# Splitting the last inner chunk and the last LayerNorm into 352 and 192 tokens instead of 256 and 288

## What is computed

```python
ALPHA = (2.0 * DEPTH) ** 0.25
def layer_norm(x, g, b):
    mu = jnp.mean(xf, axis=-1, keepdims=True)
    var = jnp.mean(jnp.square(xf - mu), axis=-1, keepdims=True)
    return (xf - mu) * lax.rsqrt(var + LN_EPS) * g + b
def squared_relu_mlp(x, w_up, w_down):
    return jnp.square(jax.nn.relu(x @ w_up)) @ w_down
...
xp = layer_norm(ALPHA * xp + mp, ln1_g[i], ln1_b[i])
xp = layer_norm(ALPHA * xp + squared_relu_mlp(xp, mlp_w_up[i], mlp_w_down[i]), ln2_g[i], ln2_b[i])
```

## Time and profile before

| | us |
|---|---|
| three runs | 1057.39, 1058.70, 1059.36; median 1058.7 |
| the profiled execution | 1058.65 |
| its span in the profile | 1056.8 |
| PE busy (share of the span) | 1040.4 (98%) |
| DVE busy | 839.9 (79%) |
| ACT busy | 661.7 (63%) |
| POOL busy | 226.9 (21%) |

### The profile page before, as it was taken

The page is one execution under the profiler, slowest core; times in us unless marked ns, Lnnn a source line. Parts: engine busy times, 40 slices in busy tenths (PEclk is TensorE's granted clock), DMA queues, the critical chain, the costliest instruction groups (busy, mean ns, idle before and its releaser), DMA issues.

```text
span 1056.8 us, 20704 instructions
## 1 busy us (share of the span) xinstructions
PE 1040.4 (98%) x8247; PEld 1017.4 (96%) x8247; DVE 839.9 (79%) x1283; ACT 661.7 (63%) x1159; POOL 226.9 (21%) x285
## 2 busy tenths in 40 slices
PE   8999999999999999999999999999999999999996
PEld 8999999999999999999999878999999999999995
DVE  6999898979779697696974664888879697696885
ACT  5999858665736647463666775675836647457432
POOL 2111032011111111103344564210111111111023
PEclk9999999999999999999999999999999999999997
DMA  7423214477877877865131211164777977878402
GB/s 256 121 91 100 81 60 138 104 159 160 176 167 159 200 160 160 203 174 185 40 121 47 67 58 39 41 180 81 159 169 158 199 161 161 201 162 175 134 12 75
DMA packets 54479, 139.83 MB, mean 132 GB/s; under 512 B 5632, under 2 KB 21440, under 8 KB 54368
## 3 DMA queue, kind: packets, MB, share of 16 engines
q0 software_dynamic: 14512, 53.60, 29.5%
q1 hardware_dynamic: 39584, 84.32, 23.9%
q10 hardware_dynamic: 288, 0.59, 0.2%
HBM read 135.95 MB, written 3.56 MB: 132 GB/s over the span
## 4 chain that ended last, share of the span: by engine, by line
PE 81%; DVE 9%; ACT 5%; issue 3%; POOL 1%; DMA 1%; SPq 0%; DVEq 0%; ACTq 0%; POOLq 0%
PE bank L2472 8%; PE bank L2491 8%; PE bank L2493 8%; PE bank L2473 8%; PE bank L2474 8%; PE bank L2492 8%; PE bank L2217 5%; PE bank L2218 5%; PE bank L2219 5%; PE bank L2304 3%; PE bank L2305 3%; PE bank L2306 3%; DVE w_lo L1348 2%; PE bank L2612 1%; PE bank L2586 1%
## 5 line engine op out<-in xcount | busy, mean ns | idle before, releaser
L834 ACT ACTIVATE w_hi<-stage 128x1024 fp32r<-128x1024 f32 x164 | 168.2, 1053 | 125.4 <-DMA stage<-w_up 67.8
L1354 DVE TENSOR_TENSOR w_lo<-stage,w_hi 128x1024 fp32r<-128x1024 f32 x164 | 197.1, 1220 | 54.0 <-ACT w_hi L834 54.0
L2491 PE MATMUL bank<-part_hi,w_hi 128*128 128x272 f32 x672 | 194.7, 290 | 0.4 <-issue 0.4
L2493 PE MATMUL bank<-part_hi,w_lo 128*128 128x272 f32 x672 | 194.2, 289 | 0.0
L2492 PE MATMUL bank<-part_lo,w_hi 128*128 128x272 f32 x672 | 193.3, 288 | 0.0
L2217 PE MATMUL bank<-x_hi,w_hi 128*128 128x288 f32 (+1 forms) x496 | 145.3, 293 | 1.4 <-issue 1.0
L2218 PE MATMUL bank<-x_lo,w_hi 128*128 128x288 f32 (+1 forms) x496 | 143.7, 290 | 0.0
L2219 PE MATMUL bank<-x_hi,w_lo 128*128 128x288 f32 (+1 forms) x496 | 143.1, 288 | 0.0
L2491 PEld LDWEIGHTS bank<-part_hi,w_hi 128*128 128x128 f32 x672 | 126.4, 188 | 1.7 <-issue 0.6
L2492 PEld LDWEIGHTS bank<-part_lo,w_hi 128*128 128x128 f32 x672 | 126.7, 189 | 0.0
L2493 PEld LDWEIGHTS bank<-part_hi,w_lo 128*128 128x128 f32 x672 | 126.7, 189 | 0.0
(11 more groups left out here) (292 smaller groups left out, 2912.5 us busy)
## 6 DMA issues: line engine op xcount, KB each, us to landing
stage<-w_up SPq DMA_DIRECT2D x54, 512.0 KB, 3.7
stage<-w_down SPq DMA_DIRECT2D x52, 512.0 KB, 4.2
stage<-w_down POOLq DMA_DIRECT2D x48, 512.0 KB, 5.4
stage<-w_up POOLq DMA_DIRECT2D x44, 512.0 KB, 5.5
stage<-w_qkv SPq DMA_DIRECT2D x10, 512.0 KB, 4.5
stage<-w_x SPq DMA_DIRECT2D x8, 512.0 KB, 5.1
stage<-w_y SPq DMA_DIRECT2D x8, 512.0 KB, 3.5
stage<-w_out SPq DMA_DIRECT2D x8, 512.0 KB, 3.3
```

Source lines behind the costliest of these rows:

```text
L834: A(w_hi[:, slot_of(l, k), :], raw_of(l, c, k), ACT.Copy).then_inc(s_whi, 1)
L1354: vt.tensor_tensor(w_lo[:, s, :], raw_of(l, c, k), w_hi[:, s, :].bitcast(F32), ALU.subtract)\
L2491: mm(out, wh, xh[:, k, :], start=(fresh and k == 0), stop=False, skip_group_check=True)
L2493: ins = mm(out, wl, xh[:, k, :], start=False, stop=(k == 1), skip_group_check=True)
```

## The change

`FINAL` gives halves of 352 and 192 columns, and `span(L, h)` returns them for the last LayerNorm (`L == 3`) and for the last chunk of layer 1's MLP, which counts as `L = 2 * l + (c > 0)`; everywhere else `HALF` stays. The tiles used in that stage are new, since 352 columns do not fit the old ones: they lie over the upper halves of `m_hi` and `m_lo`, over `z` and over `sq`. The column form of the last statistics goes in two blocks of 96 tokens instead of three.

```diff
 HALF = [(0, 256), (256, TOK - 256)]
 HW = TOK - 256
+FINAL = [(0, 352), (352, TOK - 352)]
+FC, FW = FINAL[1]
+FROWS, FCOLS = 96, 2
+def span(L, h):
+    return FINAL[h] if L == 3 else HALF[h]
...
-        fin = place("fin", [96, 12], F32, t_at["u"])
-        diag = place("diag", [96, 3, 96], F32, t_at["u"] + 64)
+        fin = place("fin", [FROWS, 12], F32, t_at["u"])
+        diag = place("diag", [FROWS, FCOLS, FROWS], F32, t_at["u"] + 64)
...
+        wide = FINAL[0][1]
+        h_at, l_at = t_at["m_hi"] + m_half, t_at["m_lo"] + m_half
+        sums_f = [[place("sum_c", [128, wide], F32, t_at["z"]), place("sumsq_c", [128, wide], F32, t_at["z"] + 4 * wide)],
+                  [sums[1][0], sums[1][1]]]
+        relu_f = place("relu_f", [128, 2, wide], F32, h_at)
+        h_sq_f = place("h_sq_f", [128, 2, wide], F32, h_at + 8 * wide)
+        mean_f = place("mean_f", [128, wide], F32, h_at + 16 * wide)
+        rstd_f = place("rstd_f", [128, wide], F32, h_at + 20 * wide)
+        msq_f = place("msq_f", [128, wide], F32, l_at)
+        red_hi_f = place("red_hi_f", [128, 2, wide], F32R, l_at + 4 * wide)
+        red_lo_f = place("red_lo_f", [128, 2, wide], F32R, l_at + 12 * wide)
+        sqt_f = place("sqt_f", [128, 2, wide], F32, t_at["sq"])
+        def wide_or(L, mine, usual):
+            return mine if L == 3 else usual
...
             def down(l, c, h, w0):
-                t0 = turn_of(l, c) * 8 + 4 * h + 2
-                width = HALF[h][1]
+                t0, L = turn_of(l, c) * 8 + 4 * h + 2, 2 * l + (c > 0)
+                width = span(L, h)[1]
...
             def up(l, c, h, w0, ts=range(4)):
                 for t in ts:
                     n0 = up_unit(l, c, h, t)
                     loop_bank(l, n0)
-                    product(n0, HALF[h][1], quad_pieces(w0, t, h))
+                    product(n0, span(2 * l + (c > 0), h)[1], quad_pieces(w0, t, h, L=2 * l + (c > 0)))
...
             pe.wait_ge(s_diag, 1)
-            for b in range(3):
-                ins = mm(bank[:, root_bank, 96 * b:96 * b + 96], ones[0:96, :], diag[:, b, :], start=True, stop=True)
+            for b in range(FCOLS):
+                ins = mm(bank[:, root_bank, FROWS * b:FROWS * b + FROWS], ones[0:FROWS, :], diag[:, b, :], start=True, stop=True)
             ins.then_inc(s_finroot, 1)
```

More of the change, by code:

```diff
@@ L977, in square @@
             def square(L, h, m):
-                c0, n = HALF[h]
+                c0, n = span(L, h)
                 pos = tile_pos(L, h, m)
@@ L983, in square @@
                     act.wait_ge(s_s2, pos - 1)
-                A((sqt_late if L == 2 else sqt)[:, pos % 2, :n], acc[:, m, c0:c0 + n], ACT.Square).then_inc(s_sqt, 1)
+                A(wide_or(L, sqt_f, sqt_late if L == 2 else sqt)[:, pos % 2, :n], acc[:, m, c0:c0 + n], ACT.Square).then_inc(s_sqt, 1)
             square(0, 0, 0)
@@ L995, in norm_stats @@
             def norm_stats(L, h):
-                _, n = HALF[h]
+                _, n = span(L, h)
                 m0 = mark[("ln", L, h)]
@@ L1000, in norm_stats @@
                     act.wait_ge(s_xhat, 4 * idx)
-                A(mean[:, :n], unit(m0)[:, :n], ACT.Copy).then_inc(s_evA, 1)
+                A(wide_or(L, mean_f, mean)[:, :n], unit(m0)[:, :n], ACT.Copy).then_inc(s_evA, 1)
                 act.wait_ge(s_var, idx + 1)
-                A(rstd[:, :n], msq[:, :n], ACT.Sqrt).then_inc(s_std, 1)
+                A(wide_or(L, rstd_f, rstd)[:, :n], wide_or(L, msq_f, msq)[:, :n], ACT.Sqrt).then_inc(s_std, 1)
             def sum_hi(L, h, part):
-                _, n = HALF[h]
+                _, n = span(L, h)
                 no = sum_no(L, h, part)
@@ L1012, in sum_hi @@
                     act.wait_ge(s_redlo, no - 1)
-                A(red_hi[:, part, :n], sums[h][part][:, :n], ACT.Copy).then_inc(s_redhi, 1)
+                A(wide_or(L, red_hi_f, red_hi)[:, part, :n], sums_of(L, h)[part][:, :n], ACT.Copy).then_inc(s_redhi, 1)
             def norm_apply(L, h, beside=lambda t: None):
-                c0, n = HALF[h]
+                c0, n = span(L, h)
                 idx = 2 * L + h
@@ L1640, in norm_apply @@
                            after_root=lambda: None):
-                c0, n = HALF[h]
+                c0, n = span(L, h)
                 idx = 2 * L + h
+                mean_now, rstd_now = wide_or(L, mean_f, mean), wide_or(L, rstd_f, rstd)
                 def pair(a, t):
@@ L2068, in add_square @@
             def add_square(L, h, m):
-                _, n = HALF[h]
+                _, n = span(L, h)
                 pos = tile_pos(L, h, m)
-                s2 = sums[h][1]
-                squares = sqt_late if L == 2 else sqt
+                s2 = sums_of(L, h)[1]
+                squares = wide_or(L, sqt_f, sqt_late if L == 2 else sqt)
                 pool.wait_ge(s_sqt, pos + 1)
@@ L2451, in down @@
                     loop_bank(l, down_unit(l, c, h, m))
-                    product(down_unit(l, c, h, m), width, down_pieces(w0 + 4, m, h))
+                    product(down_unit(l, c, h, m), width, down_pieces(w0 + 4, m, h, L))
             def up(l, c, h, w0, ts=range(4)):
```

121 lines of the change are left out of this document (66 added, 55 removed).

## The result

The changed kernel took 1061.8 us, the median of six runs (1060.2 to 1063.3), against 1058.6 us for the kernel before (1057.4 to 1059.4, six runs): ratio 1.0038, 95% interval 1.0028 to 1.0048. It is slower, by 3.1 us.

What follows compares the result with a forecast made beforehand. PE, on the chain for 81% of the span, was taken as the bound. Terms 8.1 - 2.3 - 2.6 = +3.2 us on 1058.7 gave 1061.9 us, range 1061.1 to 1063.1, widened for rivals to 1059.9 to 1064.0.

Steps and rivals of the forecast that it cites:

- rival D: Second half's narrow products fall to another pace, up to 0.50 us each: +71, total up to 1135 us; chance 0.05.
- Step 1: Last chunk's first half, 256 to 352 columns: 0.161 us per product, +8.1 us (7.9 to 8.4).
- Step 2: Last chunk's second half, 288 to 192 columns: weight load holds products at 0.112 us (ends 0.090 and 0.119).
- rival A: Second half's narrow products keep the slope, 0.090 us, the load hidden: total +1.9, 1060.6 us; chance 0.13.
- Step 3: Second half: PE waits 0.8 us for the sums, about 1 us at the fourth down slab; net gain -2.3 us.
- Rival B: Second half: DVE's stretch shorter, only PE's pace and first wait count; gain -3.3, total +2.2, 1060.9 us; chance 0.14.
- Rival C: Both halves: products at 0.090 us, no wait for DVE, only the shorter tail left: 1056.1 us; chance 0.06.
- Step 4: After the last product: narrower statistics, scaling and transfer shorten the tail by -2.6 us (-2.0 to -3.1).

Runs made afterwards that it cites:

- early-up kernel: Changed kernel (352/192) with the second half's last up tile handled by DVE and ACT before the LayerNorm's last three multiplications: 1059.6 us, ratio 1.0018.
- The series 288, 304, 320, 352: Last-chunk halves of 288/256, 304/240, 320/224 (last up tile earlier) and 352/192 (changed kernel): ratios to the kernel before 0.9992, 0.9997, 0.9996, 1.0038.
- 240-column kernel: Changed kernel with second-half products padded from 192 to 240 columns, the extra results unread: 1061.2 us, ratio 1.0031 to the kernel before.
- kernel before with the early up tile: Kernel before (256/288) with only the last up tile handled ahead of the LayerNorm's last three multiplications in the second layer: ratio 1.0003.
- 304/240 with the early up tile: Against the kernel before: halves of 304 and 240 columns, last up tile ahead of the LayerNorm's last three multiplications: 1057.1 us, ratio 0.9994.

## Why the prediction came out as it did

The forecast was +3.2 us, 1061.9; the measured median is 1061.8, and from the start of the chunk to the end the profile gives +3.0. The sum is right to 0.2 us, and its large terms, the first half and the second, were each right to 0.4. Two smaller ones behind the last product were off, in opposite directions, so that the closeness is in part luck; on the chip of the experiments the medians are 4.0 us apart. The working has small slips that change nothing: the ends of its terms add up to +2.5 and +4.5 and not +2.4 and +4.4, the chances to 0.98, and the 0.75 us in the earlier trace rows with which rival D prices one plain matmul is that of two.

*Step 1, first half.* Forecast +8.1 (7.9 to 8.4), measured 30.53 - 22.83 = +7.7. The pace is 0.159 and not the 0.161 I took: the slope of 0.00045 us per column, read between 256 and 288, is too steep. From 288 to 352 it is (0.159 - 0.133)/64 = 0.0004, about one column per cycle at 2.4 GHz, and my lower end, 0.160, was the better reading. A floor that is already near at 256 columns would make the slope between 256 and 288 flatter, not steeper, so it is not the reason. Nor is it rounding: averaged over a half, the paces repeat to 0.0002 us between profiles. Why those 32 columns cost 0.014 us and the next 64 only 0.026 stays open.

*Step 2, the floor.* Forecast 0.112, measured 0.1115, and 0.112 again with 240 columns. The rows of the warm-up, eight loads of 128 columns 0.111 us apart, were the right ones to read, and the column matmuls of four widths bear out that the floor goes with the weight columns. By the Trainium skill (TensorE: Matmul & The Clock Gate, LDWEIGHTS (loading the stationary operand)) a load of 128 columns takes 107 ns; the 112 ns between products agree to 5. The same page's fast weight load (Weight-path perf modes) would have let a load of this split type hide behind 0.090, if the type counted as not FP32; the traces speak against it, at 192, 224 and 240 columns. That was rival A, and the pace alone refutes it.

*Step 3, the waits.* The sums of the first half were ready at 1025.27, +3.4 (forecast +3.5); PE went on with the next up tile at 1025.75, +3.85, exactly as forecast. It waited in two pieces, since the high parts of the token sums can be multiplied before those of the squares are there. DVE's stretch began at +4.0 (forecast about +4.25) and took 12.8 us (forecast 12.7), piece by piece: statistics 1.37 (1.42), centring 3.21 (3.21), up tile 0.73 (0.73), reciprocal and first multiplication 3.19 (3.25), up tile 0.98 (0.91), three multiplications 2.41 (2.40), up tile 0.90 (0.82). The last low part was there at +16.8 (+17.0), PE at +15.9 (+15.95), the wait 0.96 (about 1). The half gained 2.4 us; the forecast was 2.3. Rival B needed a DVE stretch 1 us shorter; the stretch was not, and the early-up kernel showed what B would have been: no wait, 1.06 us less. Rival C needed both a pace of 0.090 and no wait, and got neither; rival D's pace appeared nowhere.

*Step 4, the tail.* Up to SP's seeing the last landing I forecast -2.6 and the profile has -3.1. Against the earlier trace rows and the timeline behind them: accumulate -0.09 (-0.10), mean matmul -0.16 (-0.16), column matmuls -0.69 (-0.68), diagonal -0.10 (-0.10), spreading and centring up to the scaling -0.81 (-0.41), scaling and last scale together -0.90 (-0.84), transfer -0.35 (-0.3). The first mis-sized term is the spreading: I priced it at half clock, and the clock stayed full. That was the end of -3.1 which the prediction names, though not for the reason given there (fewer one-column matmuls ahead): in the second profile of the same kernel the clock fell, and the tail was 0.35 us longer.
The other error is the path. I let the tail end with DVE's last scale and shift and the transfer. From SP's seeing the landing to the last instruction it is then 2.61 us before and 3.41 after, 0.8 us for which I had no term. The rows point to another path: in all twelve profiles the span ends 6.77 or 6.78 us behind POOL's last scale and shift, whatever the landing does. POOL's rows, before and after:

```profile
1048.78 1.24 POOL L2147 TENSOR_SCALAR acc<-acc,vecs 128x288 f32<-128x288 f32 x2 [6.95 <-DVE acc L2033]
...
1050.85 0.98 POOL L2185 TENSOR_SCALAR acc<-acc,vecs 128x192 f32<-128x192 f32 x2 [5.03 <-DVE acc L2071]
```

They end at 1050.02 and 1051.83, the spans at 1056.8 and 1058.6. POOL starts its two tiles when the first of DVE's four scalings is done, so only that one scaling (-0.20) and POOL's two operations (-0.26) count, -0.45 from the start of the scaling on, where I had -1.14 for four scalings, the last scale and shift and the transfer. Up to the scaling it is -1.85, where I had -1.45. Net, the tail is -2.3 us, and the forecast's -2.6 was close because these two errors, 0.4 and 0.7 us, met.

What then made the change slower than its arithmetic: the two halves together have the same 544 columns, and on one straight line of pace over width they would have cost PE the same. The line through 288 and 352 gives 0.133 - 96 x 0.0004 = 0.094 us at 192 columns, so the floor costs 192 x (0.1115 - 0.094) = 3.4 us. The wait for the low part adds 1.0 and the longer pause at the sums 0.7 (1.30 us between products there, 0.61 before). These are 5.1 of the 5.3 us by which both halves grew (7.7 - 2.4); against them stand the 2.3 us of the shorter tail. (The longer pause holds 0.16 us that the four wider sum matmuls themselves take.) The series 288, 304, 320, 352 shows it in order: from the chunk on 63.1, 63.5 (63.1 without the wait), 64.1 and 67.2 us (66.1 without the wait).

## What to carry to other kernels

Moving columns from the last, exposed piece to a piece before it pays only as long as the small piece still streams longer than its weights take to load; find the load's pace in the trace (here 0.111 us for 128 columns, in the warm-up) before choosing the width, and stop at it. When PE gets faster in a stretch, look for the engine that was 2 us ahead of it there: here DVE, whose LayerNorm work had grown by 2 us while PE's time over it shrank. A wait of that kind can be taken away by order alone (the late consumer's input ahead of work that nobody waits for), and that order costs nothing where there is no wait. And before pricing what stands behind the last product, look in several profiles for the engine whose last work keeps a fixed distance to the end; what ends after it need not be on the path.

## What the runs showed of the hardware

*The floor is flat, and goes with the weight columns.* Split products with 128 weight columns start 0.111 to 0.112 us apart with 192, 224 and 240 moving columns, 0.119 with 256, 0.133 with 288, 0.140 with 304, 0.146 with 320 and 0.159 with 352. Plain float matmuls with one moving column start 0.085, 0.098, 0.105 and 0.112 us apart with 96, 112, 120 and 128 weight columns.

*The clock behind the last product falls at different places in the same kernel.* For the spreading matmuls of the changed kernel 0.69 us in one run and 1.17 in another; of the kernel before 1.60, 1.48 (with the early up tile) and 1.10 us for six. That is 0.4 to 0.5 us of scatter in a single profile, more than several of the terms above.

*The end.* From the end of POOL's last work to the end of the span it is 6.77 to 6.78 us in twelve profiles, with last halves of 288, 256, 240, 224 and 192 columns. In the trace the instructions with which the engines meet at the end come first on POOL, 6.59 us behind its last work, and within 0.14 us behind that on the others. From SP's seeing the last landing to the last instruction it is, by contrast, 2.61 us with 288 columns (three profiles), 2.89 to 2.90 with 256, 2.87 to 2.88 with 240, 3.14 with 224 and 3.40 to 3.41 with 192 (four profiles). So the landing keeps no fixed distance to the end, which speaks against the end waiting for it; nor does the last work of ACT and DVE (5.3 to 5.7 us to POOL's instruction). What POOL does in the 6.6 us is not in the records: all engines are idle, and the windows show no transfer under way. No run gave POOL less to do there or had it done earlier, so that this would shorten the kernel is not shown.

*What differs ahead of the chunk.* The last chunk began between 990.9 and 993.6 us in 12 profiles, though the work before it is the same. Two of the latest, the 240-column kernel (992.97) and the kernel before with the early up tile (993.24), were behind from the first 9 us on, and 1.5 to 2.0 us behind the others at 17 us. Their views of ACT there show why: the next activation waits for a transfer of the input. The first row is from the kernel before with the early up tile,

```profile
8.48 0.63 ACT L856 ACTIVATE x_hi<-acc 128x512 fp32r<-128x512 f32 x1 [2.26 <-DMA acc<-xp_t]
```

and this from the changed kernel, where the same activation started 2.1 us earlier:

```profile
6.39 0.63 ACT L887 ACTIVATE x_hi<-acc 128x512 fp32r<-128x512 f32 x1 [0.29 <-DMA acc<-xp_t]
```

The granted clock is not the reason: it was 1.00 over 8 to 12 us in the first of these and 0.60 in the 240-column kernel, and the kernel before in its first profile had 0.57 there and was at most 0.3 us behind the others at 17 us. In 304/240 with the early up tile (993.59) the like happens at about 280 us, 1.8 us in the view of waits, where ACT waits for weights:

```profile
ACT w_hi L865 <- DMA stage<-w_up: 1.8, 1, 1.8
```

where the same kernel without the order had 0.2. So single executions scatter by up to 2 us with the landing of one transfer, and medians of five to eleven runs may keep some of that; a change of 1 us is read better from the start of the stretch that it touches. Of the 1.2 us between the first two profiles, 0.3 stands at 17 us and the rest comes in steps of 0.1 to 0.3 us over the whole program; what these are is left open, but they are not in the changed part.
